# Gathered down rows for the last 128 tokens, a row copy turned on chip during the mixer, and adding scatters for the routing weights

## The reference, cut to what matters

```python
def peer_ffn(h, w_query, sub_keys, expert_down, expert_up):
    def block(xb):                                  # 128 tokens
        q = (xb @ w_query).reshape(tb, 8, 2, 64)
        s = einsum('thpd,hpnd->thpn', q, sub_keys)  # 8 heads x 2 x 128 scores
        half_s, half_i = top_k(s, 16)
        cand_s = half_s[:, :, 0, :, None] + half_s[:, :, 1, None, :]
        best_s, best_pos = top_k(cand_s, 16)        # 16 experts for each head
        idx = take_along_axis(cand_i, best_pos)     # cand_i = i0 * 128 + i1
        gw = softmax(best_s)
        u = take(expert_down, idx)                  # 128 rows of 2048 for a token
        act = gelu(einsum('thkd,td->thk', u, xb))
        vv = take(expert_up, idx)
        return einsum('thk,thkd->td', gw * act, vv)
```

## Time and profile before

| | us | share of the span |
|---|---|---|
| median of three runs | 5116.04 | |
| span of the profiled execution | 5116.4 | |
| PE busy | 4951.8 | 97% |
| POOL busy | 2703.6 | 53% |
| DVE busy | 2335.1 | 46% |
| ACT busy | 1644.8 | 32% |
| DMA moved | 841.98 MB | 165 GB/s over the span |

### The profile page before, as it was taken

One profiled execution on the slowest core, in us unless ns is written; L12 is line 12 of the kernel. 1 busy time (PEld: TensorE's weight loads), 2 busy tenths in 40 slices (PEclk: granted clock), 3 DMA queues, 4 the chain that ended last, 5 costly groups with the idle time before them and its releaser, 6 DMA issues.

```text
span 5116.4 us, 65266 instructions
## 1 busy us (share of the span) xinstructions
PE 4951.8 (97%) x24570; PEld 4262.3 (83%) x24570; DVE 2335.1 (46%) x5107; ACT 1644.8 (32%) x2183; POOL 2703.6 (53%) x1372
## 2 busy tenths in 40 slices
PE   3999999999999999899899999999999999999998
PEld 2788887888888888788688888888888999999997
DVE  6333303434444433554666799400000366676674
ACT  2322222444444442222322222222222333333333
POOL 2333333222222223343344488888885688888883
PEclk7999999999999999999999999999999999999999
DMA  9222223222222225676333333333334688888983
GB/s 347 78 87 86 85 90 139 93 86 90 96 92 98 90 95 193 246 243 247 127 110 109 119 120 121 119 123 119 121 119 135 214 309 313 316 314 314 330 313 134
DMA packets 243081, 841.98 MB, mean 165 GB/s; under 512 B 37200, under 2 KB 86480, under 8 KB 202224
## 3 DMA queue, kind: packets, MB, share of 16 engines
q1 hardware_dynamic: 129680, 562.09, 31.7%
q10 hardware_dynamic: 78432, 143.55, 8.0%
q0 software_dynamic: 34816, 134.52, 7.0%
HBM read 766.91 MB, written 71.57 MB: 164 GB/s over the span
## 4 chain that ended last, share of the span: by engine, by line
PE 58%; issue 32%; POOL 6%; DMA 2%; DVE 1%; ACT 0%; POOLq 0%; ACTq 0%; SPq 0%; DVEq 0%
PE bank L890 10%; PE bank L894 10%; PE bank L892 10%; PE bank L956 7%; PE bank L958 7%; PE bank L957 7%; POOL lo L488 6%; PE bank L573 2%; PE bank L577 2%; PE bank L575 2%; DMA half<-ada_late 2%; PE bank L587 1%; DMA R<-xT 0%; POOL R L484 0%; PE bank L909 0%
## 5 line engine op out<-in xcount | busy, mean ns | idle before, releaser
L488 POOL TENSOR_TENSOR lo<-raw,hi 128x2048 fp32r<-128x2048 f32 x168 | 772.1, 4597 | 1614.2 <-ACT hi L1015 1614.2
L498 POOL TENSOR_TENSOR lo<-raw,hi 128x1024 fp32r<-128x1024 f32 x528 | 1269.7, 2407 | 535.4 <-ACT hi L1324 529.8
L573 PE MATMUL bank<-xh,hi 128*128 128x512 f32 x2336 | 977.5, 418 | 17.1 <-POOL lo L488 9.3
L1324 ACT ACTIVATE hi<-raw 128x1024 fp32r<-128x1024 f32 x528 | 547.2, 1057 | 1255.2 <-PE bank L894 1089.6
L577 PE MATMUL bank<-xh,lo 128*128 128x512 f32 x2336 | 916.9, 392 | 0.0
L575 PE MATMUL bank<-xl,hi 128*128 128x512 f32 x2336 | 913.7, 391 | 0.0
L890 PE MATMUL bank<-xh,hi 128*128 128x512 f32 x2176 | 850.4, 391 | 8.7 <-DVE xl L1578 8.7
L892 PE MATMUL bank<-xl,hi 128*128 128x512 f32 x2176 | 847.5, 389 | 0.0
L894 PE MATMUL bank<-xh,lo 128*128 128x512 f32 x2176 | 847.4, 389 | 0.0
L956 PE MATMUL bank<-CH,hi 128*128 128x384 f32 x2048 | 692.3, 338 | 3.8 <-POOL lo L498 3.8
L958 PE MATMUL bank<-CH,lo 128*128 128x384 f32 x2048 | 686.9, 335 | 0.0
(11 more groups left out here) (316 smaller groups left out, 6315.0 us busy)
## 6 DMA issues: line engine op xcount, KB each, us to landing
raw<-stream SPq DMA_DIRECT2D x528, 512.0 KB
raw<-stream SPq DMA_DIRECT2D x168, 1024.0 KB, 4.8
half<-ada_late SPq DMA_DIRECT2D x128, 512.0 KB, 4.4
arow<-stream SPq DMA_DIRECT2D x32, 1024.0 KB, 5.5
act_d<-etile ACTq DMA_DIRECT2D x128, 256.0 KB, 2.0
G_d<-dn_zero ACTq DMA_DIRECT2D x16, 1536.0 KB, 6.6
Gt<-G_d ACTq DMA_DIRECT2D x32, 768.0 KB
cf<-act_d ACTq DMA_DIRECT2D x31, 768.0 KB
```

What stands on the lines that cost most here:

```text
L488: nc.gpsimd.tensor_tensor(lo[s][:, :], raw[s][:, :], hi[s][:, :].bitcast(F32), ALU.subtract).then_inc(raw_used[s], 1)
L498: nc.gpsimd.tensor_tensor(lo_h[slot], raw_h[h % 4], hi_h[slot].bitcast(F32), ALU.subtract).then_inc(f_lo[h % 4], 1)
L573: nc.tensor.matmul(out, hi[slot][:, w], at_k(x[0], k), start=(k == 0), stop=False, skip_group_check=True)
L1324: nc.scalar.activation(hi_h[slot], raw_h[h % 4], ACT.Copy).then_inc(f_hi, 1)
```

## The change

1. **The turned copy.** `expert_down` lies in `stream` with the width on the partitions, so that a row of an expert can't be gathered from it. A new DRAM tensor `rows_d` (16384 x 2048) is filled during the mixer: 256 times SP loads half a unit (512 KB), DVE turns it in four STREAM_TRANSPOSE instructions of 128 x 256 (32 x 32 blocks), and SP stores each as 128 runs of 1 KB. These "turns" are laid out as: 76 in attention and the first gates (2 for each unit), 20 in the later gates, 20 in head 0 of the delta rule (5 a unit, in one go before the unit's convolution), and 14 in each of heads 1 to 10.
2. **Down half with 384 columns.** The 128 down units are multiplied with the first 384 tokens only; the 8 query units keep 512 columns. `act_d` gets 384 columns. There are now 7 down units behind each query unit, and 72 behind the last.
3. **Gathered down rows.** The last 128 tokens are brought token by row into PSUM (32 small matmuls, `turn_tokens`, and four ACT copies). POOL gathers 128 times a row of `rows_d` for each token (1 MB each), and DVE forms 128 dot products of 2048 (`dot`), 63 of them between the steps of `choose`, 6 after it and 59 over down units 72 to 126.
4. **Adding scatters.** The sums over equal experts are gone; POOL scatters each of the 384 columns of weights with an addition into `G_d`, 84 during the choices and 300 from down unit 72 on. Softmax is done head by head.
5. **Lows by DVE.** `lo` of down units 72 to 125 is made by DVE (`rest_low`) instead of POOL. The 128 gathers of single activations are gone.

```diff
-PER_Q = 3
+PER_Q = 7
+TURN_A = 2 * 38
+TURN_G = 2 * 10
+TURN_0 = 2 * 10
+TURN_H = 14
+LAST_TURN = 10
+LOW_FROM, LOW_TO = B_REST + 8, B_REST + 62
+Q_PUTS = 84
...
+        def unit_of_dot(k):
+            if k < query_dots:
+                return (1 + k // PER_DOTS) * (1 + PER_Q) + 2 + k % PER_DOTS * 0.8
+            if k < query_dots + EARLY_DOTS:
+                return U_Q + 2.3 + (k - query_dots) * 0.8
+            return LOW_FROM - 1 + next(n for n in range(n_busy) if sum(rest_dots[:n + 1]) > k - query_dots - EARLY_DOTS)
+        def gather_unit(k):
+            return 8.6 if k < DBUF else unit_of_dot(k - DBUF) + 0.8
+        def put_unit(n):
+            if n < Q_PUTS:
+                return 20 + n * (U_Q - 20) / Q_PUTS
+            return LOW_FROM - 1 + (n - Q_PUTS) * n_busy / (TD * P - Q_PUTS)
...
+            def turn_store(q, c, f):
+                e = 0 if isinstance(q, int) and q < TURN_A else 1
+                for b in range(4):
+                    sp.wait_ge(t_done, q * 4 + (b + 1))
+                    at_row = c * P + b * 32
+                    dst = rows_d[at_row:at_row + 32, :] if isinstance(c, int) else rows_d[bass.ds(at_row, 32), :]
+                    sp.dma_start(dst.rearrange("j (a g r) -> g a j r", a=4, g=2)[f], turn_out[e][b][:, :]
+                                 ).then_inc(t_out[b], 16)
...
+            for u in range(B_DN + 4):
+                load((u + 2) // 2, u % 2)
...
+                if u >= B_DN:
+                    turns(TURN_A + TURN_G + (u - B_DN) * TURN_0 // 4, TURN_0 // 4)
...
+                if k >= DBUF:
+                    pool.wait_ge(v_dot, k - DBUF + 1)
+                pool.indirect_dma_start(drow[k % DBUF][:, :], None, rows_d,
+                                        bass.IndirectOffsetOnAxis(ap=idx_dn[:, k:k + 1], axis=0)
+                                        ).then_inc(row_full[k % DBUF], 16)
...
-                pool.indirect_dma_start(each_g, bass.IndirectOffsetOnAxis(ap=at_g[:, n:n + 1], axis=0),
-                                        gsum[:, n:n + 1], None).then_inc(g_put[n % 4], 16)
+                if h and e == 0:
+                    pool.wait_ge(g_put[t], h * TOPK * 16)
+                pool.indirect_dma_start(each_g, bass.IndirectOffsetOnAxis(ap=at_g[:, t, at:at + 1], axis=0),
+                                        GW[:, t, at:at + 1], None, compute_op=ALU.add).then_inc(g_put[t], 16)
...
             for h in range(2 * U_DOWN):
-                low_half(h, h % 4)
+                if h not in lows_by_dve:
+                    low_half(h, h % 4)
+                while k < P and gather_unit(k) <= h / 2 - 1.7:
+                    gather_down(k)
+                    k += 1
+                while n < TD * P and put_unit(n) <= h / 2 - 1.7:
+                    put_weights(n)
+                    n += 1
...
-                    nc.tensor.matmul(out, hi[slot][:, w], at_k(xh, k), start=(k == 0), stop=False,
+                    nc.tensor.matmul(out, hi[slot][:, w], xh[:, k, 0:cols], start=(k == 0), stop=False,
...
+            def turn(q, c, f):
+                e = 0 if isinstance(q, int) and q < TURN_A else 1
+                dve.wait_ge(t_in[f], c * 16 + 16)
+                for b in range(4):
+                    if not isinstance(q, int) or q:
+                        dve.wait_ge(t_out[b], q * 16)
+                    v.transpose(turn_out[e][b][:, :].rearrange("p (k r) -> p k r", r=32),
+                                turn_in[e][f][:, :].rearrange("p (k b r) -> p k b r", b=4, r=32)[:, :, b, :]
+                                ).then_inc(t_done, 1)
...
                 for j in range(4):
-                    if not first:
-                        delta_part(h - 1, 1 - p, j)
+                    if first:
+                        for q in range(TURN_0 // 4):
+                            turn(*half_turn(TURN_A + TURN_G + j * (TURN_0 // 4) + q))
+                    else:
+                        delta_part(h - 1, 1 - p, j, next_turn)
+                    next_turn()
...
+            def dot(k):
+                dve.wait_ge(row_full[k % DBUF], (k // DBUF + 1) * 16)
+                v.scalar_tensor_tensor(drow[k % DBUF][:, :], drow[k % DBUF][:, :], 1.0, wide[:, :], ALU.mult, ALU.mult,
+                                       accum_out=dots[:, k:k + 1]).then_inc(v_dot, 1)
```

More of the change, by code:

```diff
@@ L427, in load_ada, with turn_load, turns @@
                                  ).then_inc(arow_full[n % 2], 16)
+            def turn_load(q, c, f):
+                e = 0 if isinstance(q, int) and q < TURN_A else 1
+                if not isinstance(q, int) or q >= 2:
+                    sp.wait_ge(t_done, q * 4 - 4)
+                if isinstance(q, int) and q == 0:
+                    sp.wait_ge(s_h, KT)
+                if isinstance(q, int) and q == TURN_A:
+                    sp.wait_ge(s_pv, 4 * AH)
+                cols = slice(f * HALF, (f + 1) * HALF)
+                if isinstance(c, int):
+                    src = stream[down_at(c), :, cols]
+                else:
+                    src = stream[bass.ds(c + (S_DOWN - 2 * PH), 1), :, cols].rearrange("a p n -> (a p) n")
+                sp.dma_start(turn_in[e][f][:, :], src).then_inc(t_in[f], 16)
+            def turn_store(q, c, f):
[6 more added lines that the diff above has]
+                                 ).then_inc(t_out[b], 16)
+            def turns(first, n, ahead=True):
+                for q in range(first, first + n):
+                    turn_store(*half_turn(q))
+                    if q + 2 < (TURN_A if q < TURN_A else 256):
+                        turn_load(*half_turn(q + 2))
             for s in range(2):
@@ L877, in _, with ffn_product @@
                 norm_tile(2, k, bank[7])
-            def ffn_product(slot, turn, between=None, ready=None, after=None):
-                out = bank[slot][:, :]
+            def ffn_product(slot, turn, between=None, ready=None, after=None, cols=ND):
+                out = bank[slot][:, 0:cols]
                 pe.wait_ge(*((f_bank[slot], turn) if after is None else after))
@@ L1129, in _ @@
                 gate(n // 2, n % 2)
+            for b in range(4):
+                act.wait_ge(t_out[b], TURN_A * 16)
             with act.Fori(3, U_GA // 2) as i:
@@ L1375, in take_scores, with keep_tokens, exps_of @@
                 ins.then_inc(q_s, 1)
+            def keep_tokens(part):
+                act.wait_ge(x_tr, part + 1)
+                for b in range(2):
+                    at = (2 * part + b) * P
+                    ins = nc.scalar.activation(
+                        wide[:, :].rearrange("p (a k r) -> p k a r", a=4, k=KT)[:, 8 * part + 4 * b:8 * part + 4 * b + 4, :, :],
+                        bank[2 + b][:, :].rearrange("p (k a r) -> p k a r", k=4, a=4), ACT.Copy)
+                ins.then_inc(x_tok, 1)
+            def exps_of(h):
+                act.wait_ge(q_nb, h + 1)
+                of_head = slice(h * TOPK, (h + 1) * TOPK)
+                nc.scalar.activation(ex[:, :, of_head], ex[:, :, of_head], ACT.Exp).then_inc(q_e, 1)
             for h in range(PH):
@@ L1948, in choose @@
                 step.sync()
-                for half, dst in ((0, I1), (1, I2)):
+                for half in range(2):
                     n = TT * TOPK
@@ L1966, in _ @@
+            dve.wait_ge(q_s, 1 + ONE)
+            places = cand2[:, 0, 0:P]
+            step(v.tensor_tensor(places, ident, iota, ALU.mult))
+            step.sync()
+            step(v.tensor_reduce(pcol[:, 0:1], places, AX.X, ALU.add))
+            step.sync()
+            for t in range(TD):
+                step(v.tensor_scalar(tokens[:, t, :], pcol[:, 0:1].to_broadcast([P, TOPK]), float(t * P), None, ALU.add))
+            step.sync()
             for h in range(PH):
                 choose(h)
-            dve.wait_ge(q_head, PH)
@@ new lines, in rest_low @@
+            def rest_low(h):
+                dve.wait_ge(f_hi, h + 1)
+                v.tensor_tensor(lo_h[h % 4], raw_h[h % 4], hi_h[h % 4].bitcast(F32), ALU.subtract).then_inc(f_lo[h % 4], 1)
+            k = query_dots
+            for _ in range(EARLY_DOTS):
+                dot(k)
+                k += 1
+            weigh(PH - 1)
+            dve.wait_ge(q_w, PH)
+            step(v.tensor_copy(gw3[:, :], GW[:, TD, :]))
+            for u in range(LOW_FROM, LOW_TO):
+                for b in range(2):
+                    rest_low(2 * u + b)
+                for _ in range(rest_dots[u - LOW_FROM]):
+                    dot(k)
+                    k += 1
```

350 lines of the change are left out of this document (201 added, 149 removed).

## The result

| | before | after |
|---|---|---|
| median of the runs | 5115.94 us (4 runs, 5115.43 to 5116.86) | 5840.72 us (4 runs, 5835.11 to 5843.76) |
| ratio | 1 | 1.1414, interval 1.1398 to 1.143 |
| span of the profiled execution | 5116.4 us | 5832.7 us |
| DVE's clearing of `dn_zero` (attention and gates are behind it) | 836.7 us | 1046.0 us |
| PE's first matmul of the down half | 2498.3 us | 3296.7 us |

The change made the kernel 14% slower. I had said 4897 us, and the dearest of my rivals ended at about 5200. The three starts tell the places: the mixer grew by 798 us, the down half shrank by 82 us where I expected 308, and the up half is what it was. (By PE's first matmuls the mixer ends at 2498 us before, and not near 2540 as said ahead of the prediction.)

The account below looks back on a forecast made before the run. PE, busy 97% of the span, was taken as the bound: 5116.4 - 323.5 + 4 (small matmuls) + 50 (heads 1 to 10) + 30 (head 0) + 8 (attention and gates) + 12 (down-half collisions) = 4896.9 us; 8-in-10 range 4830 to 4990.

Parts of the forecast that it names:

- the dearest of my rivals: Adding scatters in POOL's queue at 2.2 us each would end at about 5200 us; 5% chance.
- attention and gates: Mixer, 96 turns, two a unit of 12 us: 8 us lost, bounds 0 and 40.
- head 0: Delta rule's first head, 20 turns: PE waits for DVE, loss 22 to 38 us, taken as 30.
- heads 1 to 10: Delta rule, 14 turns each: 4.1 us a head plus 0.9 for late transfers, 50 us in ten, bounds 15 and 110.
- What PE saves: Down half: 6144 matmuls go from 512 to 384 columns at the up half's pace, saving 323.5 us.
- Rival 4: Weight loads set the pace at 384 columns: 235 us saved instead of 323, ending at 4985 us; 3% chance.
- What transposes and loads cost: Mixer, turns on DVE at 1.4 us each: 8 us in attention and gates, 30 in head 0, 50 in heads 1 to 10.
- zero slack: Heads 1 to 10: at three places a head, a DVE turn stands before work that PE awaits with no slack.
- rival 2: Mixer: turns stand still behind POOL's `lo`, or the DMAs are full; 4979 us; 27% chance.
- the one sentence on the store: Mixer: waits for a turn's load or earlier store priced by DMA rate, 86 to 95% full; 0.9 us a head.
- scatters still at 1.0 us: Down half, POOL: a sign expected in the profile after, adding scatters taking as long as plain ones.
- rival 3: POOL's adding scatter is dear: 0.6 us more each uses up some 230 us of gain, ending slower; 5% chance.

Follow-up runs that it names:

- e1_rows_given: The changed kernel without its turns (no loads, transposes or stores); down rows by token come from a host input. 5033.48 us, ratio to before 0.9842.
- e5: The changed kernel with the turns' loads and transposes but no stores of turned rows; down rows come from a host input. 5115.98 us, ratio 1.0002.
- e4: The changed kernel with each turn's four stores split by partition quadrant, all after the fourth transpose, instead of by block. 5442.22 us, ratio 1.0645.
- e2: The changed kernel without turns, down rows from the host, and plain scatters, so weights of experts chosen twice are not summed. 4827.21 us, ratio 0.9435.
- e11: The changed kernel with stores split by quadrant, a second output tile set, turns in delta-rule heads 1 to 8 only, down rows from the host. 5248.83 us.
- e3: The kernel before with one edit: its 384 scatters of summed weights add into `G_d` instead of writing. 5285.91 us, ratio 1.0333.
- e13: The changed kernel with stores split by partition quadrant and plain scatters, without sums over experts chosen twice. 5234.57 us, ratio 1.0234.

## Why the prediction was wrong, step by step

PE's waits in the mixer came at the places that I had named, in other sizes. The sizes, with e1_rows_given as the base; the head lengths are the distances between the starts of DVE's `output` (L1945 in after), 67.7 us in e1 and before:

| term | predicted | e5, no stores | e4, 16 engines | after |
|---|---|---|---|---|
| attention and gates | 8 | -2 | 49 | 210 |
| head 0 | 30 | 32 | 98 | 144 |
| heads 1 to 10 | 50 | 51 | 258 | 446 |
| a head of these | 72.7 | 73.2 | 95.5 | 116.1 |
| PE busy in such a head | | 68.4 | 75.9 | 77.8 |
| PE idle in such a head | | 4.8 | 19.7 | 38.3 |

(Attention: `dn_zero` at 835.6, 833.2, 884.8, 1046.0 us in e1, e5, e4 and after. Head 0: from there to the first `output`, 106.0, 137.6, 203.8, 249.9. The last three lines are means of seven full intervals; in e1 PE is busy 67.2 and idle 0.5 us of such a head.)

**What PE saves, right.** In e2 1469 matmuls fit in the 256 us from 3100, against the 1474 of the up half from which I took the pace. The whole down half takes 1218.8 us against 1506.7 less 323.5, plus 4 and 12: 1199. Of the 20 us more, 12 are waits for lows (17.6 + 6.9 where I had 12); the rest was not followed up. Rival 4, weight loads, is out.

**What transposes and loads cost, right.** 81 us for 88, and head 0 and heads 1 to 10 each within 2 us. PE's waits in e5, over the ten heads and head 0, are 24 us more than before at L890, 15 at L931, 9 at L926 and 0.4 at L898, where I had 14, 14, 11 and 2 for the ten. So the zero slack read from the earlier trace rows, and the price of a turn from the earlier trace rows, hold. One reading was off without doing harm: a head lasts 67.7 us, not 62.4, since the 998 us of the earlier trace rows are fewer than 16 heads; with 67.7 my own sum gives 311 GB/s and not 329. A transpose never stood still behind POOL's `lo`: its longest is 0.45 us. So the first half of rival 2 is out; its lateness came, but not by POOL and not by a full DMA system.

**The step that failed** is the one sentence on the store: "A turn may also wait for its load or for the store before it, and for that the DMAs count". I divided all bytes by the rate of all 16 engines, came to 86 to 95% full, and charged 0.9 us a head. It cost 42.9 us a head (116.1 - 73.2), and the same division by sixteen engines stands behind the 30 us of head 0 (144) and the 8 us of attention and gates (210). The runs separate two parts.

First, how many engines a store runs on. A turn's store has the pattern 4 x 32 x 256. In the packet records of after the stores are 131072 packets of 1 KB at 46.8 ns. From 1280 to 1536 us four of them are in flight for 44% of the time, five for 15%, more than six hardly ever and none for 26%; in e4 up to sixteen and more are. What follows is an estimate, since a packet's record does not name its engine. 56 stores a head, 1.36 us each as measured between transposes, fill four engines for 76 us; their share of the loads, (4.2 + 7.3)/16 = 0.72 MB at 1 KB/46.8 ns, is 33 us more: 109 us of a head of 116. So the four engines had next to nothing left while the mean share of sixteen stood at 0.53. The Trainium skill, "DMA: Bandwidth & Descriptors", section "Why a DMA increments its semaphore by 16 and not by 1", gives the rule: the number of engines is the largest up to 16 that divides the slowest dimension, of those that are not 1, of both patterns. By that rule 4 x 32 x 256 runs on 4 and 32 x 4 x 256 on 16; the trace and e4 agree. It speaks against this change and was not weighed. 116.1 - 95.5 = 20.6 us a head, 18.6 of them idle time of PE; over the mixer 397 us.

Second, the round trip. With one set of output tiles a turn can't begin before the stores of the last one have landed: 1.4 us of transposes, 1.9 of issue, 2.4 of landing. At 14 turns in 67.7 us there are 4.8 us for each, less DVE's other work. 95.5 - 73.2 = 22.3 us a head, of which 14.8 are idle time of PE and 7.5 its slower matmuls; a second set gave 11.4 of the 22.3 back (e11: busy 72.8, idle 11.3). Of the 10.9 us that e11 still has over e5, 4.4 are slower matmuls. Whether the other 6.5 come from SyncE's queue with its four stores and a load for each turn, or from the loads that stand behind stores on it (218.8 us of DVE's waits are for loads there), no run here tells; it stays open.

PE's idle time costs again, a term that the sum did not have: the granted clock of those stretches is 0.82 where e5 has 0.99, L689's matmul of 512 columns takes 439 ns on the mean, in e1 418, and over the mixer it comes to the 175 us above.

**The down half.** The step that failed: "scatters still at 1.0 us". The adding scatter takes 1.57 to 1.63 us on the mean in every run that has it. That was rival 3, with 5% and the right arithmetic: 0.6 us more each is 230 us in all and "uses them up", the 230 us of gain that were left. Measured: 0.59 us more each (e3), and 225 us of the down half's 308. What I held against it, that the number of descriptors is the same, does not fit the packets, 112 more a scatter; why POOL needs the time no run shows. I took the plain one's time for an operation that the trace did not show, and bounded it at 0.25 us more. POOL at 8.3 of 8.34 us a unit, which I had read myself, left no room for any error in this price; it needs some 11.6 (5.44 x 1.87 + 1.07 x 1.3).

The sum with the two losses as measured is 5116.4 - 307.5 + 225 (down half) + 798.4 (mixer) = 5832.3; the span is 5832.7. It comes out because both are read from the same starts; what bears it out are e1, e2 and e13, which take the losses away one by one.

## What to carry to other kernels

Count DMA engines before bytes: a transfer with a short outermost dimension keeps most of them idle, and a mean share of 0.5 can be four engines near their limit. Where DVE reuses a tile that a DMA reads, price the whole round trip (issue of all parts, landing) against the distance between uses, not the bytes against the bandwidth. And where an engine is read as full, an operation of its that the trace does not show decides the case: measure it by itself (one edit in the kernel before, e3, gave it) or let the range reach to twice its nearest relative. And a wait of PE costs more than its length where it lowers the clock: beside 628 us of idle time stood 175 us of slower matmuls in the mixer, and beside 158 us 47 in the down half.

## What the runs showed of the hardware that was not expected

- A scatter through POOL with an addition: 1568 ns beside 978 for the plain one, 112 packets more, with the DMA engines at a share of 0.43 or 0.74.
- Stores of one size and one run length, 128 KB in runs of 1 KB: over sixteen engines the turn's loads beside them land in 4.9 us (median), over four in 7.1, and PE's 1 MB weights in 6.9 and 8.5, with none of either in the mixer 4.8.
- STREAM_TRANSPOSE of 128 x 256 in 4-byte elements takes 0.41 us on the mean without stores and 0.44 with them, and the longest of 1024 is 0.45: 266 of them overlap a `lo` of POOL, and none is held up. The choice's product of two SBUF tiles, 1219 ns in the earlier trace rows, took 1225 to 4666 ns in after, median 3720; what held it up was not tested.
